# Stick-breaking pairs: scores and soft part four units ahead, scan and exponent three, and an earlier first matrix product

## The reference

```python
def sb_attend(q, k, v, pos_q, pos_k):
    z = jnp.einsum('bqhd,bkhd->bhqk', q, k).astype(jnp.float32) * (HEAD_DIM ** -0.5)
    before = pos_k[None, :] < pos_q[:, None]
    log_beta = jnp.where(before, jax.nn.log_sigmoid(z), NEG_INF)
    log_rest = jnp.where(before, jax.nn.log_sigmoid(-z), 0.0)
    later = lax.cumsum(log_rest, axis=log_rest.ndim - 1, reverse=True) - log_rest
    a = jnp.exp(log_beta + later)
    return jnp.einsum('bhqk,bkhd->bqhd', a.astype(v.dtype), v)
```

```python
    z = h @ w_in
    ...
    logf = jax.nn.log_sigmoid(f_logit.astype(jnp.float32) + b_f.astype(jnp.float32))
```

## Time and profile before

| what | value |
|---|---|
| median of 3 runs | 1479.09 us (1476.92 to 1482.16) |
| the profiled execution, its own time | 1475.89 us |
| its span, first to last instruction | 1473.8 us |
| PE busy | 1202.0 us, 82% of the span |
| DVE busy | 674.3 us, 46% |
| ACT busy | 430.6 us, 29% |
| POOL busy | 228.4 us, 15% |
| mean granted TensorE clock | 0.925 of 2.4 GHz |

### The profile page before, as it was taken

How to read it: one execution, slowest core, us unless ns; L and a number is a source line. 1 busy time by engine, 2 the same in 40 slices (tenths; PEclk the granted TensorE clock), 3 DMA queues, 4 the chain that set the end, 5 groups by cost and what they waited for, 6 DMA issues and landing times. The chain is left out here.

```text
span 1473.8 us, 24136 instructions
## 1 busy us (share of the span) xinstructions
PE 1202.0 (82%) x8148; PEld 830.6 (56%) x8148; DVE 674.3 (46%) x1859; ACT 430.6 (29%) x981; POOL 228.4 (15%) x366
## 2 busy tenths in 40 slices
PE   6887898997894998787769699999989499878770
PEld 4766677775773555344346466777567355444430
DVE  4455654444654353222263356555665535322226
ACT  3555664444310211011122244444530121111111
POOL 1111112222112232221110000000001223211123
PEclk9999999999995999889979899999999599999995
DMA  4212123411619999999670120000041999999975
GB/s 165 75 61 74 30 96 104 162 53 46 255 75 380 361 367 371 386 371 382 267 251 1 45 119 16 15 30 15 2 162 45 391 368 363 357 375 390 388 286 193
DMA packets 61381, 290.80 MB, mean 197 GB/s; under 512 B 12688, under 2 KB 23120, under 8 KB 44256
## 3 DMA queue, kind: packets, MB, share of 16 engines
q1 hardware_dynamic: 49408, 265.90, 48.8%
q0 software_dynamic: 10560, 18.90, 4.0%
q10 hardware_dynamic: 1312, 4.72, 0.8%
HBM read 275.91 MB, written 29.29 MB: 207 GB/s over the span
## 5 line engine op out<-in xcount | busy, mean ns | idle before, releaser
L1756 PE MATMUL psum<-w_gu,moe_xgT 128*64 128x256 f32 x1968 | 260.7, 409 | 70.3 <-DMA w_gu<-in_w_gate_up 49.8
L1756 PEld LDWEIGHTS psum<-w_gu,moe_xgT 128*64 128x64 f32 x1968 | 153.5, 146 | 161.3 <-issue 116.5
L199 PE MATMUL psum<-x_hi,ab_w_hi 128*128 128x288 f32 x384 | 126.6, 330 | 7.4 <-ACT ab_k_tok L723 4.7
L1804 ACT ACTIVATE moe_silu<-psum 64x256 f32<-64x256 f32 x64 | 24.2, 378 | 338.2 <-PE psum L1756 293.9
L1829 DVE COPY moe_xgT<-psum 128x512 f32<-128x512 f32 x64 | 44.3, 692 | 168.0 <-PE psum L1746 167.1
L201 PE MATMUL psum<-x_hi,ab_w_lo 128*128 128x288 f32 x384 | 116.1, 302 | 0.0
L200 PE MATMUL psum<-x_lo,ab_w_hi 128*128 128x288 f32 x384 | 116.0, 302 | 0.0
L1703 POOL DMA_INDIRECT y_d<-mix,moe_slots x60 | 55.5, 925 | 363.0 <-DVE mix L1842 352.2
L1773 PE MATMUL psum<-w_dn,moe_hidT 128*64 128x512 f32 x352 | 85.1, 604 | 2.2 <-issue 2.2
L199 PEld LDWEIGHTS psum<-x_hi,ab_w_hi 128*128 128x128 f32 x384 | 75.1, 196 | 13.6 <-issue 11.8
L1837 DVE COPY moe_hidT<-psum 128x128 f32<-128x128 f32 x64 | 18.7, 292 | 140.1 <-PE psum L1764 138.6
(11 more groups left out here) (305 smaller groups left out, 2162.3 us busy)
## 6 DMA issues: line engine op xcount, KB each, us to landing
w_gu<-in_w_gate_up SPq DMA_DIRECT2D x54, 2048.0 KB, 35.1
w_dn<-in_w_down SPq DMA_DIRECT2D x44, 1024.0 KB, 36.2
xT<-in_w_down SPq DMA_DIRECT2D x20, 1024.0 KB, 40.2
w_gu<-in_w_gate_up SPq DMA_DIRECT2D x10, 1536.0 KB, 39.7
w_gu<-in_w_out SPq DMA_DIRECT2D x4, 2048.0 KB, 8.7
combine_ys<-y_d SPq DMA_DIRECT2D x16, 512.0 KB, 8.5
xT<-in_w_gate_up SPq DMA_DIRECT2D x10, 512.0 KB, 42.4
xT<-cum_d SPq DMA_DIRECT2D x8, 544.0 KB, 7.1
```

The costliest lines, as they stand in the source:

```text
L199: nc.tensor.matmul(dst, r32(ah), r32(bh), start=first, stop=False)
L1756: last = nc.tensor.matmul(gu(s)[h * CB:(h + 1) * CB, 0:EH], xgT[:, s, j, :], gate_up_tile(k.w_gu[n], j)[:, h * EH:(h + 1) * EH], start=(j ...
```

## The change

`SB_LEAD` becomes 4: in sb pairs, `scores`, `soften` and `softplus` run four units ahead of `turn`, and `stick`, both masks' second pass and `exponent` three. The heads of the engines' orders grow by one unit to match. The gates' matrix gets a semaphore of its own (`wf_in`), and `products` waits for that one alone. x is loaded in four parts of 576 KB with a semaphore each. The bias and the past log gates are issued behind the first weight tile, and their users wait for two loads (32), not three (48).

```diff
--- before.py
+++ after.py
@@ -60,7 +60,7 @@
 WIDTH = [hi - lo for lo, hi in KEY_RANGE]
 EVEN, ODD = max(WIDTH[0::2]), max(WIDTH[1::2])
 ROOM = 2 * (EVEN + ODD)
-SB_LEAD, LEAD = 3, 4
+SB_LEAD, LEAD = 4, 4
 
 SCORE_BANK = [0, 1, 2, 3, 0, 1, 2, 3, 0, 2]
 
@@ -232,7 +232,8 @@
         self.id_i = room_b[:, at:at + 2 * NT].bitcast(I32).rearrange("p (c t) -> p c t", c=2)
         at += 2 * NT
         self.bf = room_b[0:HEADS, at:at + 1]
-        self.xt_in = [sem("xt_in0"), sem("xt_in1")]
+        self.xt_in = [sem(f"xt_in{n}") for n in range(4)]
+        self.wf_in = sem("wf_in")
         self.f_in, self.filled, self.consts, self.z_ready, self.act_step, self.dve_step = (
             sem(n) for n in ("f_in", "filled", "consts", "z_ready", "act_step", "dve_step"))
         self.out, self.tok_t, self.tok_e, self.cum_ready, self.x_hi_done, self.x_lo_done = (
@@ -243,13 +244,14 @@
 
     def load(self, sp):
         k = self.k
-        sp.dma_start(self.wf, k.w_f).then_inc(self.f_in, 16)
-        for b in range(2):
-            sp.dma_start(k.xT[:, 4 * b:4 * b + 4, 0:T], k.x_t[:, 4 * b:4 * b + 4, :]).then_inc(self.xt_in[b], 16)
-        sp.dma_start(self.bf, k.b_f).then_inc(self.f_in, 16)
-        sp.dma_start(self.logf[:, SEQ:NEW_AT], k.logf_past).then_inc(self.f_in, 16)
+        sp.dma_start(self.wf, k.w_f).then_inc(self.wf_in, 16)
+        for b in range(4):
+            sp.dma_start(k.xT[:, 2 * b:2 * b + 2, 0:T], k.x_t[:, 2 * b:2 * b + 2, :]).then_inc(self.xt_in[b], 16)
         for n in range(3):
             sp.dma_start(k.wp[n][:].rearrange("p j n -> p (j n)"), k.w_ab[n]).then_inc(k.wp_in[n], 16)
+            if n == 0:
+                sp.dma_start(self.bf, k.b_f).then_inc(self.f_in, 16)
+                sp.dma_start(self.logf[:, SEQ:NEW_AT], k.logf_past).then_inc(self.f_in, 16)
 
     def store(self, sp):
         k = self.k
@@ -295,10 +297,10 @@
 
     def products(self, pe):
         nc, k, z = self.nc, self.k, self.z
-        pe.wait_ge(self.f_in, 48)
+        pe.wait_ge(self.wf_in, 16)
         for j in range(J):
-            if j % 4 == 0:
-                pe.wait_ge(self.xt_in[j // 4], 16)
+            if j % 2 == 0:
+                pe.wait_ge(self.xt_in[j // 2], 16)
             nc.tensor.matmul(z[:, 0:SEQ], self.wf[:, j, :], k.xT[:, j, 0:SEQ], start=(j == 0), stop=(j == J - 1))
             last = nc.tensor.matmul(z[:, SEQ:T], self.wf[:, j, :], k.xT[:, j, SEQ:T], start=(j == 0), stop=(j == J - 1))
         last.then_inc(self.z_ready, 1)
@@ -318,15 +320,15 @@
 
     def split_x_hi(self, act):
         for j in range(J):
-            if j % 4 == 0:
-                act.wait_ge(self.xt_in[j // 4], 16)
+            if j % 2 == 0:
+                act.wait_ge(self.xt_in[j // 2], 16)
             split_hi(self.nc, self.k.x_hi[:, j, :], self.k.xT[:, j, 0:T]).then_inc(self.x_hi_done, 1)
 
     def logs(self, act):
 
         steps = Steps(act, self.act_step)
         act.wait_ge(self.z_ready, 1)
-        act.wait_ge(self.f_in, 48)
+        act.wait_ge(self.f_in, 32)
         steps.then(self.nc.scalar.activation(self.t_abs, self.z, ACT.Abs, bias=self.bf))
         steps.then(self.nc.scalar.activation(self.t_exp, self.t_abs, ACT.Exp, scale=-1.0))
         self.nc.scalar.activation(self.t_ln, self.t_exp, ACT.Ln, bias=1.0).then_inc(self.act_step, 1)
@@ -341,7 +343,7 @@
 
         v, steps = self.nc.vector, Steps(dve, self.dve_step)
         logf, low, t_ln, cum, ones = self.logf, self.low, self.t_ln, self.cum, self.ones
-        dve.wait_ge(self.f_in, 48)
+        dve.wait_ge(self.f_in, 32)
         dve.wait_ge(self.act_step, 1)
         steps.then(v.tensor_scalar(low, self.z, self.bf, 0.0, ALU.add, ALU.min))
         dve.wait_ge(self.act_step, 3)
@@ -943,8 +945,8 @@
                     if kind == "sb":
                         for u in range(SB_LEAD):
                             softplus(p, u)
-                        stick(p, 0)
-                        stick(p, 1)
+                        for u in range(SB_LEAD - 1):
+                            stick(p, u)
                     else:
                         if kind == "fox":
 
@@ -961,8 +963,8 @@
                     copies(-1)
                     for u in range(UNITS):
                         if kind == "sb":
-                            if u + 2 < UNITS:
-                                stick(p, u + 2)
+                            if u + SB_LEAD - 1 < UNITS:
+                                stick(p, u + SB_LEAD - 1)
                             if u + SB_LEAD < UNITS:
                                 softplus(p, u + SB_LEAD)
                         else:
@@ -1019,9 +1021,9 @@
                             return
                         for u in range(SB_LEAD):
                             cut(p, u, "rest_done", 0.0, "masked")
-                        cut(p, 0, "scored", NEG, "logit_ready")
-                        cut(p, 1, "scored", NEG, "logit_ready")
-                        for u in range(2, UNITS):
+                        for u in range(SB_LEAD - 1):
+                            cut(p, u, "scored", NEG, "logit_ready")
+                        for u in range(SB_LEAD - 1, UNITS):
                             cut(p, u, "scored", NEG, "logit_ready")
                             if u + 1 < UNITS:
                                 cut(p, u + 1, "rest_done", 0.0, "masked")
```

## The result

The changed kernel takes 1484.91 us (median of 20 runs, 1479.85 to 1488.74) against 1480.14 us before (20 runs). The ratio is 1.0033, 95% interval 1.0021 to 1.0045, that is 3 to 7 us slower. I had forecast 1476.9, a little faster, in a range of 1470 to 1483: the kernel became slower, and its time lies outside the range.

A forecast was written before the change was run, and what follows sets the result against it. PE's late start bounded the beginning; in the pairs no engine was full and a loop of PE, ACT, DVE and POOL set each step. Terms -4.7 + 0.5 + 2.0 = -2.2 us gave 1476.9 us, range 1470 to 1483.

The forecast's parts named there:

- The start: Gates' product at the kernel's start: PE begins at 5.4 instead of 10.12 us, 4.7 us less.
- The pairs without the clock: Four stick-breaking pairs: the vt wait goes, head and first half spend it; 0.1 us later a pair, +0.5 us.
- The clock: Second half of v after a long idle time: 0.9 us a pair lost at half speed, less 0.4 credited, +2.0 us.
- The credit: Ends of the stick-breaking pairs: some earlier clock falls are saved there, 0.4 us a pair.
- The one on the slow side: Clock falls before v in every pair, 3.3 us each, 13.2 in four: +9.0, 1488.1 us; chance 0.08.
- The clock stays out of it: Rival for the pairs: no clock loss, up to 1.6 us saved; -4.2 to -5.8, 1473.3 to 1474.9; chance 0.28.
- the lead pays in full: Rival for the pairs: slack absorbs the head's delay, 1.9 us won before vt each; -12.3, 1466.8; chance 0.10.
- the weak start: Rival at the kernel's start: it gives less or nothing, 1478.3 with PE at 6.8, 1481.6 without gain; chance 0.09.

The follow-up runs named there:

- e_start: Kernel before with only the change's start (whole `Gates` class), the lead still 3: 1472.01 us, ratio 0.9959 to the kernel before.
- e_warm: Changed kernel plus four zero-weight matmuls before the transposes of units 0 and 7 in each sb pair: 1473.67 us, 0.9973 to the kernel before.
- e_head_warm7: Changed kernel with unit 0's scan ahead of unit 3's softplus, plus zero-weight matmuls before unit 7's transposes: 1475.81 us, ratio 0.9973 to the kernel before.
- e_lead: Kernel before with only the change's lead (`SB_LEAD` 4), the old start kept: 1488.61 us, ratio 1.0077 to the kernel before.
- e_vcopy_split: Kernel before with the change's start, ACT's v copy ahead of unit 9's exponent, next k weights' split one step later: 1464.64 us, ratio 0.9914.
- e_head: Changed kernel with unit 0's scan, and POOL's masks likewise, ahead of unit 3's softplus: 1477.43 us, ratio 0.9984 to the kernel before.

## Why the prediction was wrong

**The start: right in kind, 4.7 forecast.** PE began at 5.64 rather than 5.4 and was done 5.6 us sooner; the first scores came 4.1 us sooner in the changed kernel and 4.9 in e_start. The term holds, with some luck: of the 4.1 us 4.5 are the earlier start, 1.1 the shorter slow stretch and -1.6 the fall of the clock in the v product, and the last two weren't in my sum. The rule of the Trainium skill (page "DMA: Bandwidth & Descriptors", section "Bandwidth"), by which smaller transfers would have cost 0.5 us, isn't borne out: quarters of 576 KB, queued one behind the other, came 1.50 us apart, at the rate of the halves. That page of the Trainium skill has its rule from transfers issued on GpSimd; these are issued on SP.

**The pairs without the clock: +0.5 forecast, about +0.8 measured.** T0 moved by 1.38 us in the mean (1.36 forecast), though the waits in front of it differed more from pair to pair than the few tenths that I had claimed (0.25 to 1.14 us before). (The split of v's weights came at 109.71, forecast 109.7, but by chance: the second pair began 1.7 us sooner than in the trace of before, and q's slow half took 1.6 back.) From T1 to T7 0.6 us were added (forecast: 22.9 us, measured 22.78). The wait before T7 was 2.26 (2.4 forecast), the tail won 2.04 us. Take the slow stretches out of the pair of 47.9 us, 9.1 us in four, and 45.6 are left against 45.4. e_warm, where these stretches really ran fast, has 46.1, of which 0.4 are T0 held up by the idle matmuls (8.49 against 8.13); e_head_warm7, with the scan of unit 0 first, has 45.2.

**The clock: +2.0 forecast, +9.1 measured. This is the term that failed.** I took a third of 2.7 us a pair and credited 0.4. It had two faults. The second half of v was slow in three pairs of four, at 1.5 us each (6.29, 6.31, 6.19 against 4.76), 4.5 in all where my third of 2.7 made 3.6: the size was overrated, the frequency underrated, and the two errors nearly cancel. And I priced one place only, which is the fault that counts. I wrote that the head's idle time would grow to about 2 us, saw a queue delay in it, and never asked what it does to the clock. It grew to 3.13, 3.27 and 2.39 us in three pairs, where q's first half ran at the full clock for the most part and ended early, and in these three the second half of q was slow, 1.5 to 1.6 us each, 4.6 in all; in the first pair it was 1.15, and q stayed fast. That place I gave no price at all. In sum -4.1 + 0.8 + 9.1 = +5.8 us, and the traces are 5.9 apart behind the fourth pair.

**The credit.** Of the 0.4 us a pair that I gave back for falls saved at the pairs' ends, at most 0.1 to 0.2 can be seen: T8 to the next pair became 2.04 us shorter, where the wait at vt alone accounts for 1.9. The falls there did become rarer: from T8 to the next pair the mean clock was 1.00, 0.76, 0.68 and 1.00 before, and 1.00, 1.00, 0.90 and 1.00 after. But the last values wait for DVE's result copy, and a faster PE only waits longer for it (7.7 us in four, 5.9 before).

**The rivals.** The one on the slow side, the clock's fall in front of v with 1488.1 us and a chance of 0.08, named the mechanism and its place. Too dear in price (13.2 us against 4.5) and without the place in q, it came out 3 us above the measured median: that it came so near is luck, two errors against each other. It deserved far more than 0.08: the earlier trace rows showed a fall of the clock behind an idle 2.1 us, and I had worked out an idle 2.4. The rule of the Trainium skill (page "TensorE: Matmul & The Clock Gate", section "HAM oscillation — how this bites in real kernels") stood beside it, and the trace agrees with it in three pairs of four. The example on that page of the Trainium skill has waits of 3 to 5 us, longer than those here. "The clock stays out of it", with 0.28, fell by the two slow places and by e_warm, "the lead pays in full" by e_head_warm7, the weak start by e_start.

What stays open: which idle time brings a fall and which doesn't. The wait before T7 was 2.24 to 2.27 us in all four pairs, and v was slow after three of them; in e_lead after two. The length of the wait before T0 doesn't decide it either: q was slow after 2.39 us in the changed kernel and after 2.21 in e_vcopy_split, and fast after 2.44 and 2.39 in that same kernel. I have not found what sets them apart, and one profiled execution for each kernel is too little for it.

## What to carry to other kernels

When a change moves PE's idle time, ask what PE does right behind it: 2 us of idleness can halve the clock for the next matmuls, and that price, here 1.5 us most times and 2.9 twice, is paid in full only where those matmuls are on the path. An idle time in front of work that waits anyhow is cheap (the kernel before had its slow stretches there); the same idle time in front of a long product is not. The mean clock doesn't show this: 0.93 and 0.92 over the four pairs. And a wait that ends on a copy queued behind another engine's late result was mended more cheaply here by exchanging the two in that queue (pairs of 44.4 us) than by running everything one unit further ahead (47.9), which made each pair's head longer.

## What the runs showed of the hardware that I had not expected

Matmuls with nothing but zeros as weights hold the clock: about 2 us of them in each of the two idle times kept it at 2.4 GHz through q's and v's second halves in all four pairs (e_warm), and a kernel with more work was 9 us faster than one with less. And a slow stretch can cover the whole of a product's half: in e_lead and e_head one pair took 7.66 and 7.67 us from T7 to T8, 2.9 above the undisturbed 4.76, about the full 2.7 of 24 matmuls at half speed. In e_lead every stretch of 2 us from 182 to 188 is at 1.2 GHz, and in e_head every one from 126 to 132.
